# One stream of gate products laid between the products of three token mixers, and a merge that reads raw logits

## The chip, the cores and the metric

The kernel runs on one core of one Trainium2 chip. Its metric is the device time of one execution in microseconds (us). Five engines work side by side: PE (TensorE, matrix products), DVE (VectorE), ACT (ScalarE), POOL (GpSimd) and SP (SyncE, which here does nothing but issue transfers). They meet at semaphores only. SBUF is the on-chip memory and PSUM the accumulator memory that PE writes.

## The reference

One layer of a decoder trunk on 1024 tokens of width 1024, in f32. `h` is a normalised and modulated `x`; one projection `w_in` gives the inputs of four mixers and the logits of four gates; each mixer's output goes through its own branch weight, is gated and summed:

```python
h = rms_norm(x, g_mix[l]) * (1.0 + sc1) + sh1
(a_q, a_k, a_v, conv_in, c_q, c_k, c_v, c_r, c_low,
 d_q, d_k, d_v, gate_logits) = jnp.split(h @ w_in[l], split_points, axis=-1)
y_a = dilated_attention_mixer(a_q, a_k, a_v, q_gain[l], k_gain[l]) @ w_br_a[l]
y_b = conformer_conv_mixer(conv_in, ...) @ w_br_b[l]
y_c = gla_mixer(c_q, c_k, c_v, c_r, c_low, ...) @ w_br_c[l]
y_d = stick_breaking_mixer(d_q, d_k, d_v) @ w_br_d[l]
gates = jax.nn.sigmoid(gate_logits).reshape(bsz, seq, N_BRANCH, D_MODEL)
merged = (gates[:, :, 0] * y_a + gates[:, :, 1] * y_b
          + gates[:, :, 2] * y_c + gates[:, :, 3] * y_d)
x = x + gt1 * (merged @ w_out[l])
h = rms_norm(x, g_mlp[l]) * (1.0 + sc2) + sh2
x = x + gt2 * (jnp.square(jax.nn.relu(h @ w_up[l])) @ w_down[l])
```

The gate logits are 4 x 1024 columns, that is 32 tiles of 128 columns by 1024 tokens. The conv mixer has 256 channels, GLA 4 heads of 128 values with chunks of 64, stick-breaking 4 heads of 64, the dilated attention 3 groups of 4 heads of 64.

## The kernel before, in words

Every stage is one or more blocks. A block has one instruction list for each engine, written out by hand in the order in which it runs, and a barrier stands between two blocks: no engine begins the next block before all have left the last. So the order of the work is the order of the code, and a wait on a semaphore holds back all that stands behind it on its engine.

A product that has to be as exact as f32 is made of three f32r matmuls: both factors are split into a high and a low part, and `split_product` (L610) issues high x high, low x high and high x low. A dense tile is 128 columns of `w_in` (512 KB) times all of `h`. Its path is: SP loads it, ACT copies it to the high part (L132), POOL subtracts to get the low part (L136), PE makes two halves of 512 tokens with 8 x 3 = 24 matmuls of 128x512 each, ACT copies each half out of PSUM (L153), SP stores it. The class `Dense` does this for the 39 tiles of the projections during the front stage (0 to 506.5 us), with rings of two.

The stages then are, with their stretches in the profiled execution:

- window (dilated attention), block 1, 510.6 to 564.3 us: turns v by PE transposes, and for each of 12 tiles of q and k: squares on POOL, sums over the head on PE (into `ps_n`), ACT Ln (L1395) and Exp (L1398) into `wa_rinv`, DVE multiplies q or k by it (L1444). Ahead of the loop ACT is told which table of functions to load (L1389, `preload_act_table_set`).
- block 2, to 654 us: 24 units; 11 of them have two key tiles, 13 have one. PE: scores (L1493), transposes of the probabilities (L1504), values (L1514).
- block 3 (merging), 654.3 to 694.8 us: DVE merges the three groups, PE transposes, the result goes to `mix` in DRAM. Beside it two gate tiles (class `LastGates`).
- GLA: prepare to 738.8 us, with two more gate tiles; eight levels of masked products to 806.5 us (4 groups of 16 matmuls a level, L1889; two products and four masked copies a level on DVE, L1916, L1917, L1928); the state over 8 chunk pairs to 837.3 us; the norm to 873.0 us, for each head ACT L2023 (Square), L2024 to L2026 (Exp, Ln, Exp for the output gate), L2028 and L2029 (Ln, Exp of the mean square), and PE sums with `ones`.
- stick-breaking, 873.0 to 1036.1 us: a short block that turns v and scales q, then 24 steps, one for each half of the queries, key tile and head pair. A step has scores (L2136), sums with `ones` times an accumulated `later` (L2153) and with `reach` (L2156), values (L2170); DVE copies, adds to `later`, takes the argument; ACT makes Abs, Exp, Ln and a last Exp.
- merge, 1036.1 to 1467.0 us: for n = 0 to 7 and i = 0 to 3, PE makes the gate tile (48 matmuls, for the 28 tiles that no mixer has made) and then the branch product y (60 matmuls for one n over the four i); ACT takes the sigmoid from PSUM (L781), DVE multiplies and adds (L884, L889, L891), `merged` goes to DRAM. The branch weights of one n are loaded, split on ACT (L769) and POOL (L825).
- tail, from 1467 us: output product and MLP.

`recycle_semaphores` makes all semaphores free again and has barriers of its own.

Of the kernel before, what the change touches and what calls it, by code (L numbers as in the profile page):

```python
# [5 lines left out]
F32 = mybir.dt.float32  # L6
# [7 lines left out]
P = 128  # L14
# [60 lines left out]
class Dense:  # L75
# [3 lines left out]
    def __init__(self, nc, k, ctx, w_in):  # L79
# [16 lines left out]
        self.tiles = conv + stick + low + linear + window  # L96
        self.early = len(conv)

# [56 lines left out]
    def store(self, sp, j, h):  # L155
        column, width, row = self.tiles[j]
        sp.wait_ge(self.copied, NH * j + h + 1)
        sp.dma_start(self.k.proj[row * P:row * P + width, h * HALF:(h + 1) * HALF], self.out[0:width, h, :]).then_inc(self.stored[h], 16)
# [10 lines left out]
def stage_front(nc, k, dense, x, c, w_ada, b_ada, g_mix, g_mlp, conv_w, conv_b, ln_g, ln_b, b_gate, o_gain, q_gain, k_gain):  # L169
# [4 lines left out]
    N_TILES = len(dense.tiles)  # L174
# [13 lines left out]
    with ExitStack() as ctx:  # L188
# [78 lines left out]
        def _(sp):  # L267
# [33 lines left out]
            for j in range(dense.SLOTS, N_TILES):  # L301
# [9 lines left out]
            for j in range(N_TILES - 2, N_TILES):  # L311
                for h in range(NH):
                    dense.store(sp, j, h)
# [4 lines left out]
        def _(pool):  # L318
# [9 lines left out]
            for j in range(OPENING, N_TILES):  # L328
                dense.low(pool, j)

        @block.scalar
        def _(act):
# [56 lines left out]
            for j in range(2 * C, N_TILES):  # L389
                for h in range(NH):  # L390
                    dense.copy(act, j, h)
                if j + 2 < N_TILES:
                    dense.split(act, j + 2)
# [231 lines left out]
class LastGates:  # L625

    def __init__(self, nc, k, ctx, name, w_in, mixers):
        self.nc, self.k, self.mixers = nc, k, mixers  # L630
        self.w_view = w_in[0].rearrange("(t p) n -> p t n", p=P)
        self.raw = ctx.enter_context(nc.sbuf_tensor(f"{name}_raw", [P, 2, KT, P], F32))
        self.hi = ctx.enter_context(nc.sbuf_tensor(f"{name}_hi", [P, 2, KT, P], F32R))
        self.lo = ctx.enter_context(nc.sbuf_tensor(f"{name}_lo", [P, 2, KT, P], F32R))
        self.out = ctx.enter_context(nc.sbuf_tensor(f"{name}_out", [P, S], F32))
        self.loaded = sems(nc, ctx, f"{name}_in0", f"{name}_in1")
        self.hi_ready, self.lo_ready, self.done, self.copied, self.stored = sems(
            nc, ctx, *(f"{name}_{s}" for s in ("hi_ready", "lo_ready", "done", "copied", "stored")))

    def load(self, sp, j):  # L640
        if j >= 2:
            sp.wait_ge(self.lo_ready, j - 1)
        column = COL_GATES + (self.mixers[j] + 1) * D - P
        sp.dma_start(self.raw[:, j % 2], self.w_view[:, :, column:column + P]).then_inc(self.loaded[j % 2], 16)
# [1711 lines left out]
```

## Time and profile before

| | us |
|---|---|
| median of three runs | 2297.35 |
| the runs | 2296.37, 2302.18, 2297.35 |
| the profiled execution | 2296.16 |
| its span (first to last instruction) | 2294.4 |
| PE busy | 2105.6 (92%) |
| DVE, ACT, POOL busy | 957.6, 621.3, 562.1 |
| mean granted clock of PE | 0.958 of full |

1.8 us of the profiled execution lie outside its span. Busy time of PE is not its work: an f32r matmul of 128x512 is recorded with 0.39 us while the next one starts much earlier, so a stretch that is "busy" is one in which matmuls stand close together. The starts tell the pace. PEclk is the clock that was granted, as a share of 2.4 GHz; 0.5 is 1.2 GHz.

### The profile page before, as it was taken

The numbers are of one execution on the slowest core, as the hardware profiler recorded it, in microseconds if no ns is written. First come the engines' busy times: TensorE is split into PE (matmuls) and PEld (weight loads), VectorE is DVE, ScalarE is ACT, GpSimd is POOL, SyncE is SP. The second block draws the span as 40 slices with busy tenths as digits, with TensorE's granted clock in tenths as the row PEclk, the third lists the DMA queues.
The fourth block names the chain that finished last, engine by engine and source line by source line (L and its number), as shares of the span: only waits on it lengthen the run. The fifth ranks groups of instructions, "written<-read, shape, count | busy, mean of one in ns | idle before, by whom it ended". The sixth has DMA issues, their size and how long they took to land. (4 is left out here: it accounts for less than half of the span.)

```text
span 2294.4 us, 23961 instructions
## 1 busy us (share of the span) xinstructions
PE 2105.6 (92%) x9584; PEld 1666.5 (73%) x9584; DVE 957.6 (42%) x1146; ACT 621.3 (27%) x853; POOL 562.1 (24%) x258
## 2 busy tenths in 40 slices
PE   6999999986977676888999999689999999999999
PEld 5878888763865643326888888568888888888887
DVE  6365671018655924663111111345333333333334
ACT  5311111225732243553111111232222112122111
POOL 0212222216002400102222221120434334334332
PEclk9999999999988876998999999899999999999999
DMA  8345543233133011005222221340111111111112
GB/s 278 95 139 161 165 134 92 87 111 137 34 109 139 1 55 74 1 12 176 58 57 57 57 57 57 119 156 19 47 46 46 56 46 46 56 46 46 56 46 92
DMA packets 187865, 187.43 MB, mean 82 GB/s; under 512 B 7370, under 2 KB 154954, under 8 KB 187770
## 3 DMA queue, kind: packets, MB, share of 16 engines
q1 hardware_dynamic: 187600, 186.03, 25.7%
q8 instruction: 67, 1.10, 0.2%
q14 instruction: 28, 0.23, 0.0%
q10 hardware_dynamic: 170, 0.07, 0.0%
HBM read 148.17 MB, written 37.91 MB: 81 GB/s over the span
## 5 line engine op out<-in xcount | busy, mean ns | idle before, releaser
L617 PE MATMUL dn_ps<-h_hi,dn_hi 128*128 128x512 f32 (+1 forms) x608 | 240.5, 396 | 5.0 <-DVE h_lo L532 5.0
L619 PE MATMUL dn_ps<-h_hi,dn_lo 128*128 128x512 f32 (+1 forms) x608 | 237.3, 390 | 0.0
L618 PE MATMUL dn_ps<-h_lo,dn_hi 128*128 128x512 f32 (+1 forms) x608 | 237.1, 390 | 0.0
L1274 DVE TENSOR_TENSOR tl_x<-tl_x,tl_bank 128x512 f32<-128x512 f32 x256 | 173.3, 687 | 133.0 <-PE tl_bank L619 133.0
L1110 POOL TENSOR_TENSOR tl_w_lo<-tl_raw,tl_w_hi 128x1024 fp32r<-128x1024 f32 x64 | 153.5, 2399 | 228.4 <-ACT tl_w_hi L1031 228.4
L617 PE MATMUL tl_bank<-tl_h_hi,tl_w_hi 128*128 128x512 f32 x512 | 199.5, 390 | 0.0
L618 PE MATMUL tl_bank<-tl_h_lo,tl_w_hi 128*128 128x512 f32 x512 | 199.2, 389 | 0.0
L619 PE MATMUL tl_bank<-tl_h_hi,tl_w_lo 128*128 128x512 f32 x512 | 199.2, 389 | 0.0
L617 PE MATMUL tl_bank<-tl_w_hi,tl_u_hi 128*128 128x512 f32 x512 | 199.2, 389 | 0.0
L618 PE MATMUL tl_bank<-tl_w_lo,tl_u_hi 128*128 128x512 f32 x512 | 199.2, 389 | 0.0
L619 PE MATMUL tl_bank<-tl_w_hi,tl_u_lo 128*128 128x512 f32 x512 | 199.2, 389 | 0.0
L617 PE MATMUL mg_ps_g<-h_hi,mg_hi 128*128 128x512 f32 x448 | 175.4, 392 | 16.9 <-POOL mg_lo L822 16.9
L618 PE MATMUL mg_ps_g<-h_lo,mg_hi 128*128 128x512 f32 x448 | 175.2, 391 | 0.0
L619 PE MATMUL mg_ps_g<-h_hi,mg_lo 128*128 128x512 f32 x448 | 175.2, 391 | 0.0
L1116 POOL TENSOR_TENSOR tl_u_lo<-tl_square,tl_u_hi 128x1024 fp32r<-128x1024 f32 x32 | 104.5, 3266 | 277.2 <-DVE tl_square L1264 277.2
L136 POOL TENSOR_TENSOR dn_lo<-dn_raw,dn_hi 128x1024 fp32r<-128x1024 f32 (+1 forms) x37 | 87.4, 2365 | 327.7 <-ACT dn_hi L132 327.7
L1264 DVE TENSOR_TENSOR tl_square<-tl_relu 128x1024 f32<-128x1024 f32 x32 | 39.7, 1239 | 306.4 <-ACT tl_relu L1062 306.4
L822 POOL TENSOR_TENSOR mg_lo<-mg_raw,mg_hi 128x1024 fp32r<-128x1024 f32 x28 | 67.2, 2400 | 344.3 <-ACT mg_hi L763 344.3
L1031 ACT ACTIVATE tl_w_hi<-tl_raw 128x1024 fp32r<-128x1024 f32 x64 | 67.8, 1061 | 286.2 <-PE tl_bank L619 226.7
L617 PEld LDWEIGHTS dn_ps<-h_hi,dn_hi 128*128 128x128 f32 (+1 forms) x608 | 112.9, 186 | 31.0 <-DVE h_lo L532 6.2
L153 ACT ACTIVATE dn_out<-dn_ps 128x512 f32<-128x512 f32 (+1 forms) x74 | 44.3, 598 | 331.0 <-PE dn_ps L619 331.0
L889 DVE TENSOR_TENSOR mg_gate<-mg_ps_y,mg_gate 128x1024 f32<-128x1024 f32 x24 | 29.4, 1225 | 245.6 <-PE mg_ps_y L619 245.6
(313 smaller groups left out, 3900.0 us busy)
## 6 DMA issues: line engine op xcount, KB each, us to landing
ada<-w_ada_dram SPq DMA_DIRECT2D x24, 1024.0 KB, 7.5
dn_raw<-w_in_dram SPq DMA_DIRECT2D x38, 512.0 KB, 4.4
proj<-dn_out SPq DMA_DIRECT2D x72, 256.0 KB, 2.3
tl_raw<-w_up_dram SPq DMA_DIRECT2D x32, 512.0 KB, 3.8
tl_raw<-w_down_dram SPq DMA_DIRECT2D x32, 512.0 KB, 3.8
mg_raw<-w_in_dram SPq DMA_DIRECT2D x28, 512.0 KB, 4.6
wa_qk<-proj SPq DMA_DIRECT2D x6, 1024.0 KB, 17.4
mg_y_raw<-mix SPq DMA_DIRECT2D x10, 512.0 KB, 3.6
```

The source lines that it names most:

```text
L136: self.nc.gpsimd.tensor_tensor(self.lo_at(j), self.raw_at(j), self.hi_at(j).bitcast(F32), ALU.subtract).then_inc(self.lo_ready, 1)
L153: self.nc.scalar.activation(self.out[0:width, h, :], self.ps[0:width, h, :], ACT.Copy).then_inc(self.copied, 1)
L617: nc.tensor.matmul(out, w_hi[:, t, :], x_hi[:, t, :], start=begin, stop=False)
L618: nc.tensor.matmul(out, w_hi[:, t, :], x_lo[:, t, :], start=False, stop=False)
L619: mm = nc.tensor.matmul(out, w_lo[:, t, :], x_hi[:, t, :], start=False, stop=end)
L822: nc.gpsimd.tensor_tensor(g_lo[:, i % 2], g_raw[:, i % 2], g_hi[:, i % 2].bitcast(F32), ALU.subtract).then_inc(g_lo_ready, 1)
L889: nc.vector.tensor_tensor(gate[:, i % 2], y, gate[:, i % 2], ALU.mult).then_inc(gated, 1)
L1031: nc.scalar.activation(dst, raw[:, ring(j)], ACT.Copy).then_inc(hi_ready, 1)
L1110: nc.gpsimd.tensor_tensor(lo, raw[:, ring(j)], hi.bitcast(F32), ALU.subtract).then_inc(lo_ready, 1)
L1116: nc.gpsimd.tensor_tensor(u_lo[:, b % 2, f, :], square[:, n % 2], u_hi[:, b % 2, f, :].bitcast(F32), ALU.subtract).then_inc(u_lo_ready, 1)
L1264: nc.vector.tensor_tensor(square[:, n % 2], relu[:, n % 2], relu[:, n % 2], ALU.mult).then_inc(square_ready, 1)
L1274: nc.vector.tensor_tensor(x1[:, tt, cols], x1[:, tt, cols], bank[:, 4 + n % 4, :], ALU.add).then_inc(summed, 1)
```

## The change

All 32 gate tiles become tiles of `Dense`, behind the 39 of the projections, and are cut into pieces: a half is three pieces of 9, 9 and 6 matmuls (3, 3 and 2 of the 8 row tiles). `pieces(pe, n)` issues the next n of them, `serve` does ACT's part for a number of halves (the split of the next tile, the copy of this half), `lower` POOL's, `move` SP's (load the tile after the next, store the half). `LastGates` goes. 64 halves are dealt out so: window 6 (prepare), 8 (units), 4 (merging); GLA 8 (prepare), 8 (levels), 2 (state), 4 (norm); stick-breaking 20; merge 4. The mixers run in the order dilated attention, GLA, stick-breaking, as before. The logits go to DRAM raw, all 4 x 1024 rows.

```diff
-        self.tiles = conv + stick + low + linear + window
+        gates = [(COL_GATES + i * D + n * P, P, None) for n in range(D // P) for i in range(4)]
+        self.tiles = conv + stick + low + linear + window + gates
...
+    PARTS = (0, 3, 6, KT)
+    def pieces(self, pe, count):
+        for _ in range(count):
+            g, part = divmod(self.piece, 3)
+            j, h = self.first_gate + g // NH, g % NH
+            if part == 0:
+                pe.wait_ge(self.lo_ready, j + 1)
+                pe.wait_ge(self.copied, NH * (j - 1) + h + 1)
+            last = self.product(self.ps[:, h, :], j, h, self.PARTS[part], self.PARTS[part + 1])
+            if part == 2:
+                last.then_inc(self.done, 1)
+            self.piece += 1
+    def serve(self, act, halves):
+        while self.served < halves:
+            j, h = self.first_gate + self.served // NH, self.served % NH
+            if h == 0 and j + 1 < len(self.tiles):
+                self.split(act, j + 1)
+            self.copy(act, j, h)
+            self.served += 1
+    def move(self, sp, halves):
+        while self.moved < halves:
+            j, h = self.first_gate + self.moved // NH, self.moved % NH
+            if h == 0 and j + 2 < len(self.tiles):
+                self.load(sp, j + 2)
+            self.store(sp, j, h)
+            self.moved += 1
```

In the window's first block, the tables are no longer preloaded and Ln and Exp work in place in PSUM:

```diff
             def _(act):
-                nc.scalar.preload_act_table_set("natural_log_exp_and_others")
                 for t in range(2 * A_TILES):
+                    dense.serve(act, FROM + min(PREPARE, HEAD // 3 + t // 3))
                     act.wait_ge(summed, t + 1)
-                    nc.scalar.activation(rinv[:, t % 2], ps_n[:, t % 2, :, :].rearrange("p h c -> p (h c)"), ACT.Ln,
-                                         scale=1.0 / E, bias=k.eps[:, 0:1]).then_inc(logged, 1)
+                    nc.scalar.activation(sums, sums, ACT.Ln, scale=1.0 / E, bias=k.eps[:, 0:1]).then_inc(logged, 1)
                     act.wait_ge(logged, t + 1)
-                    nc.scalar.activation(rinv[:, t % 2], rinv[:, t % 2], ACT.Exp, scale=-0.5).then_inc(rooted, 1)
+                    nc.scalar.activation(sums, sums, ACT.Exp, scale=-0.5).then_inc(rooted, 1)
```

PE has 6 pieces ahead of the v transposes, then one behind each group of sums. In the units one piece stands between a unit's transposes and its values, and the scores have one PSUM buffer instead of two. In the merging block the mix store stands behind all of the block's `dense.move`. In GLA each of the first three of the four groups of a level is followed by a piece, the masked products have 3 PSUM buffers instead of 4, each head of the norm is preceded by two pieces. In stick-breaking the two blocks are one; the steps run head pair by head pair, the sums stay in one PSUM accumulator to which `pass_on` adds a product with `below`, so DVE's copies and adds to `later` go, and two pieces stand in each step:

```diff
+            dense.pieces(pe, HEAD)
...
+            for n in range(N + 3):
+                if n < N:
+                    scores(n)
+                if n < N + 2:
+                    dense.pieces(pe, 1)
+                if 2 <= n < N + 2:
+                    pass_on(n - 2)
+                if 1 <= n <= N:
+                    sums(n - 1)
+                if n < N + 2:
+                    dense.pieces(pe, 1)
+                if n >= 3:
+                    values(n - 3)
```

It also gets a `preload_act_table_set` of its own. In the merge, the gate products and their chain go; the logits are loaded into a ring of three, squashed in place, and the branch weights have two buffers:

```diff
+    GATE_RING = 3
+    Y_RING = 3
...
+            def load_branch(n):
+                if n == 1:
+                    sp.wait_ge(dense.done, NH * len(dense.tiles))
+                if n >= 2:
+                    sp.wait_ge(b_lo_ready, n - 1)
...
+            def load_logits(m):
+                if m < GATE_RING:
+                    sp.wait_ge(y_lo_ready, Y_TILES)
+                else:
+                    sp.wait_ge(used, m - GATE_RING + 1)
+                sp.dma_start(gate[:, m % GATE_RING], k.logits[m * P:(m + 1) * P, :]).then_inc(g_in[m % GATE_RING], 16)
...
+            for m in range(M):
+                load_logits(m)
+                if m % 4 == 2 and m >= 6:
+                    n = m // 4 - 1
+                    sp.wait_ge(used, 4 * n + 4)
+                    sp.dma_start(k.merged[n * P:(n + 1) * P, :], merged[:, n]).then_inc(stored, 16)
+                    if n + 2 < N_TILES:
+                        load_branch(n + 2)
...
+            for m in range(M):
+                squash(m)
+                if m == 0:
+                    split_branch(1)
+                if m % 4 == 3 and 1 <= m // 4 < N_TILES - 1:
+                    split_branch(m // 4 + 1)
...
+        def _(pe):
+            dense.pieces(pe, 3 * HALVES)
+            for m in range(M):
...
+                pe.wait_ge(b_lo_ready, n + 1)
```

Two more `recycle_semaphores` are in `build`, one behind the window stage and one behind the merge.

On ACT, in the window's first block, before (`wa_ps_n` holds the sums, `wa_rinv` the result):

```order
L1389 ACT_TABLE_LOAD
L1395 ACTIVATE wa_rinv<-wa_ps_n,eps 128x1024
L1398 ACTIVATE wa_rinv<-wa_rinv 128x1024
L1395 ACTIVATE wa_rinv<-wa_ps_n,eps 128x1024
L1398 ACTIVATE wa_rinv<-wa_rinv 128x1024
```

and now:

```order
L1328 ACT_TABLE_LOAD
L1328 ACTIVATE wa_ps_n<-wa_ps_n,eps 128x1024
L1330 ACT_TABLE_LOAD
L1330 ACTIVATE wa_ps_n<-wa_ps_n 128x1024
L135 ACTIVATE dn_hi<-dn_raw 128x1024
L156 ACTIVATE dn_out<-dn_ps 128x512
L1328 ACT_TABLE_LOAD
L1328 ACTIVATE wa_ps_n<-wa_ps_n,eps 128x1024
L1330 ACT_TABLE_LOAD
L1330 ACTIVATE wa_ps_n<-wa_ps_n 128x1024
```

One table load for the block has become one ahead of each Ln and one ahead of each Exp, 24 in the block; the gate stream's split and copy stand between.

On ACT, in the norm of GLA, one head, before:

```order
L2023 ACTIVATE gn_sq<-gl_oT 128x1024
L2024 ACTIVATE gn_sig<-gl_rT 128x1024
L2025 ACTIVATE gn_sig<-gn_sig 128x1024
L2026 ACTIVATE gn_sig<-gn_sig 128x1024
L2028 ACTIVATE gn_rinv<-gn_ps,eps 128x1024
L2029 ACTIVATE gn_rinv<-gn_rinv 128x1024
```

and now (`gl_att` and `gl_q` hold what `gn_sq`, `gn_rinv` and `gn_sig` held):

```order
L1972 ACTIVATE gl_att<-gl_oT 128x1024
L1973 ACTIVATE gl_q<-gl_rT 128x1024
L1974 ACT_TABLE_LOAD
L1974 ACTIVATE gl_q<-gl_q 128x1024
L1975 ACT_TABLE_LOAD
L1975 ACTIVATE gl_q<-gl_q 128x1024
L1977 ACT_TABLE_LOAD
L1977 ACTIVATE gl_att<-gn_ps,eps 128x1024
L1978 ACT_TABLE_LOAD
L1978 ACTIVATE gl_att<-gl_att 128x1024
```

Four loads have come in for each of the four heads; two more are in GLA's first block, and in the whole program there are 52 where there were 8.

On PE, in a step of stick-breaking, before (`sb_ps_z` scores, `sb_ps_c` sums, `sb_ps_o` values):

```order
L2136 MATMUL sb_ps_z<-sb_qk 128x384 x2
L2153 MATMUL sb_ps_c<-sb_later,ones 128x256
L2156 MATMUL sb_ps_c<-sb_softplus,reach 128x384
L2153 MATMUL sb_ps_c<-sb_later,ones 128x256
L2156 MATMUL sb_ps_c<-sb_softplus,reach 128x384
L2170 MATMUL sb_ps_o<-sb_weight,sb_v_tok 64x256 x2
```

and now, a sum, a piece of six matmuls of the gate stream (`dn_ps`) behind it, the values and the next scores:

```order
L2129 MATMUL sb_ps_c<-sb_softplus,sb_below 128x384 x2
L2119 MATMUL sb_ps_c<-sb_softplus,reach 128x512 x2
L663 MATMUL dn_ps<-h_hi,dn_hi 128x512
L664 MATMUL dn_ps<-h_lo,dn_hi 128x512
L665 MATMUL dn_ps<-h_hi,dn_lo 128x512
...
L2141 MATMUL sb_ps_o<-sb_weight,sb_v_tok 64x256 x2
L2105 MATMUL sb_ps_z<-sb_qk 128x256 x2
L663 MATMUL dn_ps<-h_hi,dn_hi 128x512
```

The gate matmuls that stood in the merge stand between the products of a step; the number of the step's own products is the same.

## Rows read from the trace of the kernel before

**Rows 1.** The page's first line.

```profile
span 2294.4 us, 23961 instructions
```

**Rows 2.** Stages: length; busy of PE, PEld, DVE, ACT, POOL; PEclk, DMA share, GB/s.

```profile
510.60:564.30 53.70, 32.91 (x96) 15.40 (x97) 46.02 (x38) 27.22 (x25) 37.85 (x16) 0.88 0.45 176
564.30:651.60 87.30, 83.50 (x612) 72.11 (x612) 57.60 (x95) 61.64 (x216) 0.00 (x0) 0.96 0.10 35
654.30:694.80 40.50, 26.00 (x112) 21.37 (x112) 18.13 (x23) 4.34 (x5) 4.73 (x2) 0.79 0.47 158
694.80:738.80 44.00, 38.85 (x152) 27.60 (x152) 24.93 (x19) 15.99 (x12) 8.22 (x3) 0.82 0.40 145
738.80:806.50 67.70, 45.12 (x512) 43.98 (x512) 66.04 (x59) 13.38 (x7) 29.75 (x17) 0.87 0.00 1
806.50:837.30 30.80, 30.13 (x176) 21.74 (x176) 4.12 (x14) 4.77 (x8) 0.00 (x0) 0.94 0.19 69
837.30:873.00 35.70, 15.12 (x16) 4.69 (x16) 14.58 (x12) 25.15 (x25) 0.00 (x0) 0.55 0.15 59
873.00:1036.10 163.10, 129.46 (x384) 59.36 (x384) 91.92 (x117) 78.54 (x96) 16.09 (x32) 0.87 0.08 26
1036.10:1467.00 430.90, 417.98 (x1824) 345.31 (x1824) 87.15 (x64) 81.10 (x79) 98.29 (x36) 0.98 0.26 72
```

**Rows 3.** PE in order of time in the merge: start, us, instruction, idle before.

```profile
1043.63 0.80 PE L617 MATMUL mg_ps_g<-h_hi,mg_hi 128*128 128x512 f32 x1 [16.86 <-POOL mg_lo L822]
...
1044.65 0.63 PE L619 MATMUL mg_ps_g<-h_hi,mg_lo 128*128 128x512 f32 x1
1045.08 0.63 PE L617 MATMUL mg_ps_g<-h_hi,mg_hi 128*128 128x512 f32 x1
...
1055.06 0.39 PE L617 MATMUL mg_ps_g<-h_hi,mg_hi 128*128 128x512 f32 x1
...
1056.88 0.39 PE L619 MATMUL mg_ps_g<-h_hi,mg_lo 128*128 128x512 f32 x1
```

**Rows 4.** ACT in order of time, late in the front stage.

```profile
453.90 1.28 ACT L399 ACT_TABLE_LOAD   x1
455.19 1.12 ACT L399 ACTIVATE cv_rinv<-fr_open_ps,eps 128x1024 f32<-128x1024 f32 x1
456.33 1.28 ACT L402 ACT_TABLE_LOAD   x1
457.62 1.06 ACT L402 ACTIVATE cv_rinv<-cv_rinv 128x1024 f32<-128x1024 f32 x1
```

**Rows 5.** PE in order of time, the window's first block.

```profile
515.99 9.93 PE L1410 MATMUL wa_ps_v<-ident,wa_vT 128*128 128x128 f32 x48 [9.29 <-DMA wa_vT<-proj]
```

**Rows 6.** GLA's levels in order of time: DVE, then PE.

```profile
761.04 5.02 DVE L1928 COPY_PREDICATED gl_att<-gl_mask,gl_ps_att 128x1024 f32<-128x1024 int32 x4
...
768.17 5.02 DVE L1928 COPY_PREDICATED gl_att<-gl_mask,gl_ps_att 128x1024 f32<-128x1024 int32 x4
...
769.67 5.29 PE L1889 MATMUL gl_ps_att<-gl_parts 64*128 64x128 f32 x64 [1.72 <-DVE gl_att L1928]
```

**Rows 7.** ACT in order of time in GLA's norm, one head.

```profile
851.91 1.06 ACT L2023 ACTIVATE gn_sq<-gl_oT 128x1024 f32<-128x1024 f32 x1
...
859.07 1.06 ACT L2023 ACTIVATE gn_sq<-gl_oT 128x1024 f32<-128x1024 f32 x1
```

**Rows 8.** PE in order of time in stick-breaking, one full step.

```profile
979.84 1.12 PE L2153 MATMUL sb_ps_c<-sb_later,ones 128*128 128x512 f32 x2
...
986.39 1.12 PE L2153 MATMUL sb_ps_c<-sb_later,ones 128*128 128x512 f32 x2
```

**Rows 9.** The low part of a branch weight on POOL: ns min/median/max.

```profile
L825 POOL TENSOR_TENSOR mg_br_lo<-mg_br_raw,mg_br_hi x8: 3893/3930/3945, 1047.6 to 1447.7; 128x1280 fp32r<-128x1280 f32 x8
```

**Rows 10.** Transfers by issue, with size and us to landing.

```profile
wa_qk<-proj SPq DMA_DIRECT2D x6, 1024.0 KB, 17.4
...
mg_raw<-logits SPq DMA_DIRECT2D x4, 512.0 KB, 4.2
```

More of the change, by code:

```diff
@@ L740, in store @@
-            def store(n):
-                sp.wait_ge(added, n * 3 + 3)
-                sp.dma_start(k.merged[bass.ds(n * P, P), :], merged[:, :]).then_inc(stored, 16)
-            def load_y(t0, t1):
-                for t in range(t0, t1):
-                    if t >= 2:
-                        sp.wait_ge(y_lo_ready, t - 1)
-                    sp.dma_start(y_raw[:, t % 2], k.mix[t * P:(t + 1) * P, :]).then_inc(y_in[t % 2], 16)
-            loads(0, first=True)
-            with sp.Fori(1, N_TILES - 1) as n:
-                loads(n)
@@ L753, in _, with load_y @@
-            loads(N_TILES - 1, last=True)
-            store(N_TILES - 1)
+            def load_y(t):
+                if t >= GATE_RING:
+                    sp.wait_ge(y_lo_ready, t - GATE_RING + 1)
+                sp.dma_start(gate[:, t % GATE_RING], k.mix[t * P:(t + 1) * P, :]).then_inc(y_in[t], 16)
+            def load_branch(n):
[3 more added lines that the diff above has]
+                    sp.wait_ge(b_lo_ready, n - 1)
+                for j in range(4):
+                    sp.dma_start(b_raw[n % 2][:, Y_FIRST[j]:Y_FIRST[j + 1], :],
+                                 w_br[j][0].rearrange("(t p) n -> p t n", p=P)[:, :, n * P:(n + 1) * P]).then_inc(b_in[n % 2], 16)
@@ L896, in _ @@
-            low_y(0, Y_EARLY)
-            body(0, first=True)
-            with dve.Fori(1, N_TILES) as n:
-                body(n)
+            for t in range(Y_TILES):
+                dve.wait_ge(y_hi_ready, t + 1)
+                nc.vector.tensor_tensor(k.y_lo[:, t, :], gate[:, t % GATE_RING], k.y_hi[:, t, :].bitcast(F32), ALU.subtract).then_inc(y_lo_ready, 1)
+            for m in range(M):
+                n, i = m // 4, m % 4
+                dve.wait_ge(gate_ready, m + 1)
+                dve.wait_ge(y_done, m + 1)
+                y = ps_y[:, m % Y_RING, :, :].rearrange("p h c -> p (h c)")
+                g = gate[:, m % GATE_RING]
+                if i == 0:
+                    nc.vector.tensor_tensor(merged[:, n], y, g, ALU.mult).then_inc(used, 1)
+                else:
+                    nc.vector.tensor_tensor(g, y, g, ALU.mult).then_inc(gated, 1)
+                    dve.wait_ge(gated, m - n)
+                    dve.wait_ge(used, m)
+                    nc.vector.tensor_tensor(merged[:, n], merged[:, n], g, ALU.add).then_inc(used, 1)
@@ L1675, in _ @@
                 last.then_inc(turned, 1)
-            for j in range(2, len(GATES_IN_WINDOW)):
-                pe.wait_ge(gates.copied, j - 1)
-                gates.product(pe, j, ps_g[:, j % 2])
+            dense.pieces(pe, 3)
 GLA_HEADS = 4
@@ L1754, in _ @@
                     last.then_inc(turned, 1)
[L1755 to L1758 removed]
+                dense.pieces(pe, 3 * (PREPARE - 1) - HEAD)
                 pe.wait_ge(dve_step, 7)
```

890 lines of the change are left out of this document (396 added, 494 removed).

## The prediction

> **What bounds the kernel now.** I read the stages first. The span is 2294.4 us [rows 1], and the changed stages fill 510.6 to 1467.0 of it [rows 2]; front and tail keep their instructions. In the merge PE is busy for 417.98 of 430.90 us at a clock of 0.98, so the merge is PE's work and nothing else. In the other rows of that group PE leaves room: prepare of the window 32.91 of 53.70, levels 45.12 of 67.70, norm 15.12 of 35.70, stick-breaking 129.46 of 163.10. Then I read who fills those: DVE has 46.02 in the window's prepare and 66.04 of 67.70 in the levels, ACT 25.15 of 35.70 in the norm. The units (83.50 of 87.30) and the state (30.13 of 30.80) have no room.
>
> Next the pace of PE, from starts and not from busy time [rows 3]. At full clock (2.4 GHz) eight starts lie between 1055.06 and 1056.88, 0.2275 us for one f32r matmul of 128x512. At half clock (1.2 GHz), after 16.86 us in which PE was idle, it is 0.43 (1044.65 to 1045.08). So a half of a gate tile, 24 matmuls, is 5.46 us, a piece 1.82 on average, and a cold start costs some 2 us more, for about eleven matmuls.
>
> **What goes.** The merge loses 28 tiles x 48 = 1344 matmuls, 305.8 us. What it keeps is 480 matmuls of y, 109.2 us, and it gets 4 halves, 21.8 us, plus 2 for a cold start. At its old pace it had 415.0 us of matmuls in 430.9.
>
> New waits in the merge: body n+2 needs its branch weight, whose chain hangs on the last logits of body n+1. In body n+1 the first gated product is done 12 matmuls (2.7) and one DVE operation (1.2, estimated from the 1.25 of a masked copy of the same size, 5.02 for four [rows 6]) after its start; then the load of logits, 4.2 [rows 10] with a store and a branch weight ahead of it in the queue, so 5 to 6; a sigmoid and the split, 1.1 and 1.3 (estimates from ACT's 1.06 for 1024 elements [rows 4]); POOL 3.93 [rows 9]. Together about 15.5 after the start of the body, which is only 13.7 of matmuls long. I take 2 us for each of seven bodies, 14, and 3 for the first logits, which can be fetched only when all of y is split. The merge: 21.8 + 2 + 109.2 + 14 + 3 = 150, a change of **-281**. Below, if the chain hides, -295; above, see the rivals.
>
> **What the mixers get.** 56 more halves less what was there: they had 8 (the four early tiles) and get 60, so 52 x 5.46 = 284 us go in. What each stage can hide:
>
> - Window prepare: 6 halves, and 24 table loads on ACT. Where Ln and Exp alternate with a load before each, the trace has load 1.28, Ln 1.12, load 1.28, Exp 1.06, end to start [rows 4]: from 453.90 to 458.68, 4.8 us. Twelve tiles make 57.6, more than PE's sums (32.91 less 9.93 over twelve, 1.9 a tile [rows 2, 5]) and a piece (1.82), so ACT is the bound. It begins late: six pieces first, 10.9 plus 2 cold from 511, which hides the 9.29 wait for v; then a third of the v transposes, 3.3 [rows 5], and a tile's sums, to 529. Add 57.6 and some 4 for splits and copies of the stream: 591 in place of 564.3, **+27**. With the loads at nothing the block would be bound by PE at +17.
> - Units: 24 pieces, 43.7 us. PE is idle for 3.8 of the stretch and its clock 0.96 may rise to 1.0, worth 3.3 of 83.50 [rows 2]. 43.7 - 3.8 - 3.3 = **+37**. The single score buffer costs nothing if a piece stands in the wait for DVE; if not, it takes from the hidden part only.
> - Window merging: four halves as before. The last pieces and their store stand ahead of the mix store, 3.5, and there is one more recycling, 2 (an estimate: the gap between the blocks of the units and of the merging is 2.7 [rows 2]). **+5.5**.
> - GLA prepare: 8 halves for 4, +21.8; idle there 5.2. One or two table loads. **+18**.
> - Levels: now DVE's 7.13 (761.04 to 768.17) for a level; PE needs 5.3 of its own and 3 pieces, 5.46, and becomes the bound at 10.7 [rows 6]. The masks on DVE still hold the first copies back (761.04 less one level is 753.9, 15.1 after the start), then comes what is left of the first level, 5, and seven more: 15.1 + 5 + 7 x 10.7 = 95 for 67.7, **+27**.
> - State: six pieces between saturated products, **+11**.
> - Norm: a head takes 7.16 on ACT [rows 7]; four loads add 4 x 1.28 = 5.12, less 0.7 in which ACT now waits for the sums (7.16 less six activations of near 1.07), plus the stream's copies: 11.7 a head. Four heads, **+20**. PE's 21.8 of pieces go beside that; without the loads this stage would gain or lose about 1.
> - Stick-breaking: 20 halves, 109.2 us. A full step is 6.55 on PE [rows 8] with scores, four sums and values back to back, and the 24 steps hold 18 full steps' worth of columns, 118. Then v's transposes 3.3, about 6 for some 54 switches between the two kinds of product (0.1 each, my guess, bounds 0 and 16), 9.4 from the last product to the merge as now: 109.2 + 118 + 3.3 + 6 + 9.4 = 246, against 163.1 **+84**. From a step's scores to its sum there are two DVE operations (1.25 each) and three of ACT (1.06 each), 6 us with waking; PE has three pieces, the sums before, the values and the next scores to do in that time, 11.
> - Tail: one more recycling, **+2**.
>
> Sum: 27 + 37 + 5.5 + 18 + 27 + 11 + 20 + 84 + 2 - 281 = -49.5. Against the profiled execution, 2296.16, that is 2246.7. The median of the runs is 1.2 us above that execution, so **2248**.
>
> **A rule against it.** The rows show a load of 1.28 us and the next ACT instruction at its end, with nothing between [rows 4]. The Trainium skill, ScalarE: Activation LUTs, section What ACT_TABLE_LOAD costs, adds about 1.38 us of draining to each switch, 2.66 in all; in this trace that does not show. By it, 40 loads on the path would cost 55 us more.
> The same page, section Table sets: the hidden batching unit, says that Ln and Exp share one set, so that a pair should need one load; the program's order shows one for each all the same.
>
> **The rivals.**
>
> 1. The loads or the pieces hide better than I think. For it: ACT in the levels and in stick-breaking has room, and a load can run before its wait ends. Against it: in Ln-Exp chains there is no wait to hide in. Without the loads' cost on the path, -10 in the prepare and -18 in the norm, 2220; with two of the merge's stalls gone too, 2213. Chance 0.17.
> 2. A rival on the slow side: the ring of three logits bounds the merge. For one m, the time is (L + 4.5)/3, where L is a load's landing and 4.5 the sigmoid, two DVE operations and waking. PE needs 109.2/32 = 3.4 for one m, so it decides from L = 5.8 on, and eats the whole gain of 49.5 from L = 12: 32 x (12 + 4.5)/3 = 176, where my sum has 126. For it: 1 MB loads took 17.4 when the queue was full [rows 10]; the merge reads 0.5 MB for logits each 3.4 us plus weights and stores, near 250 GB/s. Against it: the same load took 4.2. At L = 14, 32 x 18.5/3 = 197, +71, so 2319. Chance 0.05.
> 3. Each switch costs 2.66 on the path, by the sum above: 24 and 16 loads more by 1.38, +55, so 2303: no gain. Only a stall behind each load, which the rows don't have, would do that. Chance 0.04.
> 4. The pieces break the mixers' chains: a piece is issued whole, and PE waits in it for `lo_ready` or `copied`, with the mixer's products queued behind. If ACT serves a half late by 1 us in each of the 60, +50 to +60 and the gain is gone: 2300. For it: ACT's list puts a copy behind a mixer's waits in each stage. Against: a half has three pieces of slack and two PSUM banks. Chance 0.08.
>
> **How the numbers follow.** My own case has 0.66, with 2215 to 2285. A measurement of this kernel can tell about 0.3%, 7 us, from no change. Faster by more than that: 0.17 and 0.64 of my 0.66, 0.81. Within: its last 0.02 and 0.05 of rivals 3 and 4, which end close to no change, 0.07. Slower: the other 0.07 of these and rival 2, 0.12. The range reaches past rival 1, by the bounds of the guessed terms (16 for the switches, 14 for the stalls), and up to 2290: 2205 to 2290.
>
> **What would show it.** The merge near 150 us with PE waiting for the branch weight's low part at each body; 24 loads of 1.28 between Ln and Exp and PE idle there; the levels at 10.7 a level with DVE waiting for PE; a step of stick-breaking of 10.2. I am wrong if PE stands idle within the stick steps, if a load is followed by a gap, if the logits land later than 6 us, or if the clock of the mixers stays below 0.9.

## The result: slower by 1.9%, and where the time went

The changed kernel takes 2344.79 us (median; 2342.97 to 2348.71) against 2296.86 of the kernel before beside it: the ratio is 1.0193, 95% interval 1.016 to 1.0227. It is 48 us slower where 49 us faster was forecast. The profiled execution has a span of 2346.9 us, 52.5 more than before [rows 1]; it is the slowest of the four executions, 3.9 above their median.

The page's PE line has 2139.7 us busy where it had 2105.6, and 9584 matmuls as before. The same number of products is made, so the question is where PE stood idle or ran at half clock. The view by stage says it; its columns are those of [rows 2], kernel after:

```profile
514.50:598.80 84.30, 65.93 (x240) 42.91 (x240) 26.52 (x38) 62.12 (x57) 35.87 (x19) 0.96 0.40 147
598.80:729.80 131.00, 126.64 (x804) 106.55 (x804) 62.05 (x97) 70.21 (x228) 9.57 (x4) 0.99 0.20 60
729.80:775.20 45.40, 27.42 (x112) 22.54 (x112) 18.57 (x23) 4.56 (x7) 4.79 (x3) 0.80 0.44 141
775.20:836.30 61.10, 58.88 (x248) 45.18 (x248) 22.54 (x19) 23.06 (x22) 12.61 (x5) 0.93 0.41 135
836.30:947.40 111.10, 102.55 (x704) 83.77 (x705) 72.30 (x59) 21.84 (x19) 37.90 (x21) 0.94 0.14 41
947.40:989.50 42.10, 41.21 (x224) 30.63 (x224) 4.13 (x14) 6.70 (x11) 2.36 (x1) 0.95 0.22 76
989.50:1047.70 58.20, 36.72 (x112) 24.59 (x112) 18.88 (x12) 49.64 (x46) 4.71 (x2) 0.79 0.22 72
1047.70:1346.20 298.50, 244.31 (x864) 152.59 (x864) 75.69 (x80) 99.46 (x127) 38.34 (x44) 0.89 0.16 50
1346.20:1522.30 176.10, 146.70 (x576) 117.25 (x576) 93.49 (x66) 57.20 (x56) 25.80 (x9) 0.90 0.57 185
```

Taking each stage from its first instruction to the first of the next, before and after:

| stage | before | after | change | forecast |
|---|---|---|---|---|
| front | 510.6 | 514.5 | +3.9 | 0 |
| window prepare | 53.7 | 84.7 | +31.0 | +27 |
| units | 90.4 | 130.6 | +40.2 | +37 |
| window merging | 40.1 | 45.4 | +5.3 | +5.5 |
| GLA prepare | 44.1 | 61.7 | +17.6 | +18 |
| levels | 67.6 | 110.5 | +42.9 | +27 |
| state and norm | 66.5 | 100.3 | +33.8 | +31 |
| stick-breaking | 163.6 | 298.5 | +134.9 | +84 |
| merge | 436.4 | 176.1 | -260.3 | -281 |
| tail | 821.4 | 824.6 | +3.2 | +2 |

Three stages hold 87.5 of the 102 us between forecast and result: stick-breaking (51), the merge (21) and the levels (16).

**Stick-breaking.** The view of waits of that stage names one wait of PE above all (us in total, times, longest), kernel after:

```profile
PE dn_ps L663 <- POOL dn_lo L139: 45.1, 7, 8.3
```

PE stands before a piece because the tile's low part is not there. In order of time around one of the seven (start, us, engine, instruction), kernel after:

```profile
1079.20 1.05 ACT L135 ACTIVATE dn_hi<-dn_raw 128x1024 fp32r<-128x1024 f32 x1
1079.36 0.41 POOL L2245 TENSOR_SCALAR_AFFINE_SELECT sb_weight<-sb_weight 128x256 f32<-128x256 f32 x1 [5.65 <-ACT sb_weight L2228]
...
1080.25 1.98 PE L2105 MATMUL sb_ps_z<-sb_qk 64*128 64x512 f32 x4
1080.64 0.41 POOL L2245 TENSOR_SCALAR_AFFINE_SELECT sb_softplus<-sb_softplus 128x256 f32<-128x256 f32 x1 [0.88 <-DVE sb_softplus L2182]
...
1086.67 0.61 ACT L2228 ACTIVATE sb_weight<-sb_weight 128x512 f32<-128x512 f32 x1
...
1087.35 0.41 POOL L2245 TENSOR_SCALAR_AFFINE_SELECT sb_weight<-sb_weight 128x256 f32<-128x256 f32 x1 [6.30 <-ACT sb_weight L2228]
1087.72 2.34 POOL L139 TENSOR_TENSOR dn_lo<-dn_raw,dn_hi 128x1024 fp32r<-128x1024 f32 x1
...
1090.11 0.79 PE L663 MATMUL dn_ps<-h_hi,dn_hi 128*128 128x512 f32 x1 [7.88 <-POOL dn_lo L139]
1090.70 0.63 PE L664 MATMUL dn_ps<-h_lo,dn_hi 128*128 128x512 f32 x1
```

ACT has the high part ready at 1080.25, and POOL needs 2.34 us for the low part. But POOL's list has a mask of the weights first, and that waits for ACT's Exp of a later turn of the loop, which ends at 1087.28. The low part comes 7.5 us after it could, POOL is idle for 6.30 of them, and when PE goes on its first matmuls are 0.43 to 0.59 apart where full clock has 0.2275: half clock. Six of the seven waits last 6.5 to 8.3 us; the seventh lasts 0.8, and behind it PE goes on at full clock.

**Merge.** The same pattern at a body's start, PE, then ACT, then POOL, kernel after:

```profile
1446.40 0.39 PE L665 MATMUL mg_ps_y<-y_hi,mg_br_lo 128*128 128x512 f32 x1
1451.58 0.79 PE L663 MATMUL mg_ps_y<-y_hi,mg_br_hi 128*128 128x512 f32 x1 [4.79 <-POOL mg_br_lo L775]
```

```profile
1446.34 1.06 ACT L756 ACTIVATE mg_gate<-mg_gate 128x1024 f32<-128x1024 f32 x1 [4.38 <-DMA mg_gate<-logits]
1447.31 1.25 ACT L748 ACTIVATE mg_br_hi<-mg_br_raw 128x1280 fp32r<-128x1280 f32 x1
```

```profile
1448.63 2.89 POOL L775 TENSOR_TENSOR mg_br_lo<-mg_br_raw,mg_br_hi 128x1280 fp32r<-128x1280 f32 x1 [15.90 <-ACT mg_br_hi L748]
```

The split of the branch weight stands behind the sigmoid of the last logits, and those land late: the body has ended (1446.40) before its successor's weight is split. It happens at three bodies, every second one, 4.2 to 4.8 us each with half clock behind it, and POOL's part is 2.9, where [rows 9] had 3.93. Two more waits of that size stand at the merge's start, one for the low part of y and one for DVE's first gated product (L815), which hangs on the first logits. PE's waits of the stage, kernel after:

```profile
PE mg_ps_y L663 <- POOL mg_br_lo L775: 13.7, 3, 4.8
PE dn_ps L663 <- PEq L60: 8.9, 1, 8.9
PE mg_ps_y L663 <- DVE y_lo L807: 4.8, 1, 4.8
PE mg_ps_y L663 <- DVE mg_merged L815: 4.1, 1, 4.1
```

The 8.9 is the time between PE's last piece in stick-breaking and its first in the merge, and lies in the stage before. Ahead of the wait for the low part of y, ACT stands before a copy of the gate stream, whose buffer is still being stored, with y's split behind it, kernel after:

```profile
1378.31 0.60 ACT L156 ACTIVATE dn_out<-dn_ps 128x512 f32<-128x512 f32 x1 [7.88 <-DMA logits<-dn_out]
1378.81 2.94 ACT L752 ACTIVATE y_hi<-mg_gate 128x1024 fp32r<-128x1024 f32 x3
```

**Table loads.** ACT in the window's first block, kernel after:

```profile
562.54 1.28 ACT L1328 ACT_TABLE_LOAD   x1
563.83 1.09 ACT L1328 ACTIVATE wa_ps_n<-wa_ps_n,eps 128x1024 f32<-128x1024 f32 x1
564.94 1.28 ACT L1330 ACT_TABLE_LOAD   x1
566.23 1.01 ACT L1330 ACTIVATE wa_ps_n<-wa_ps_n 128x1024 f32<-128x1024 f32 x1
567.15 0.59 ACT L156 ACTIVATE dn_out<-dn_ps 128x512 f32<-128x512 f32 x1
567.77 1.28 ACT L1328 ACT_TABLE_LOAD   x1
```

Everything is end to start as in [rows 4]; a tile takes 4.7 us, or 5.2 with a copy of the stream. There is no gap beside a load. The trace has 50 loads in the whole program, not the 52 named ahead of the prediction; 24 and 16 of them are those of this block and of the norm.

### The profile page after: what moved, and what is told of

Read it like the earlier page. It is cut to its first block and busy times, and to the rows that moved or that the text cites. A ratio compares the mean times of both kernels' runs of the same rounds, so it can differ in the third digit from the quotient of the medians.

```text
span 2346.9 us, 23858 instructions
## 1 busy us (share of the span) xinstructions
PE 2139.7 (91%) x9584; PEld 1683.4 (72%) x9584; DVE 940.5 (40%) x1109; ACT 704.8 (30%) x955; POOL 541.3 (23%) x260
## 5 line engine op out<-in xcount | busy, mean ns | idle before, releaser
L663 PE MATMUL dn_ps<-h_hi,dn_hi 128*128 128x512 f32 (+1 forms) x1120 | 479.3, 428 | 86.0 <-POOL dn_lo L139 45.1
L664 PE MATMUL dn_ps<-h_lo,dn_hi 128*128 128x512 f32 (+1 forms) x1120 | 449.5, 401 | 0.0
L665 PE MATMUL dn_ps<-h_hi,dn_lo 128*128 128x512 f32 (+1 forms) x1120 | 449.2, 401 | 0.0
L663 PEld LDWEIGHTS dn_ps<-h_hi,dn_hi 128*128 128x128 f32 (+1 forms) x1120 | 217.4, 194 | 162.4 <-issue 59.7
L139 POOL TENSOR_TENSOR dn_lo<-dn_raw,dn_hi 128x1024 fp32r<-128x1024 f32 (+1 forms) x69 | 165.2, 2395 | 721.2 <-ACT dn_hi L135 721.2
L664 PEld LDWEIGHTS dn_ps<-h_lo,dn_hi 128*128 128x128 f32 (+1 forms) x1120 | 217.7, 194 | 51.2 <-issue 7.8
L665 PEld LDWEIGHTS dn_ps<-h_hi,dn_lo 128*128 128x128 f32 (+1 forms) x1120 | 216.5, 193 | 50.7
L663 PEld LDWEIGHTS tl_bank<-tl_h_hi,tl_w_hi 128*128 128x128 f32 x512 | 96.1, 188 | 20.0
L665 PEld LDWEIGHTS tl_bank<-tl_h_hi,tl_w_lo 128*128 128x128 f32 x512 | 96.1, 188 | 20.0
L664 PEld LDWEIGHTS tl_bank<-tl_w_lo,tl_u_hi 128*128 128x128 f32 x512 | 96.1, 188 | 20.0
```

The costliest lines, as they stand in the source:

```text
L139: self.nc.gpsimd.tensor_tensor(self.lo_at(j), self.raw_at(j), self.hi_at(j).bitcast(F32), ALU.subtract).then_inc(self.lo_ready, 1)
L663: nc.tensor.matmul(out, w_hi[:, t, :], x_hi[:, t, :], start=begin, stop=False)
L664: nc.tensor.matmul(out, w_hi[:, t, :], x_lo[:, t, :], start=False, stop=False)
L665: mm = nc.tensor.matmul(out, w_lo[:, t, :], x_hi[:, t, :], start=False, stop=end)
```

## The experiments

The first four are repairs of the changed kernel, one cause each and then all three. A ratio is always to the kernel before as timed beside the run. That kernel's medians there were 2302.94 (first four), 2303.43 (next four), 2297.83 (the next two) and 2313.16 (the last two), with single executions from 2292.61 to 2322.65, and its 2296.86 above is the lowest. So gains are read from one changed kernel to the next. The changed kernel itself, timed again, came within 2.7 us, and of a difference smaller than that nothing is concluded.

**POOL's list in stick-breaking.**

```diff
             for n in range(N + 1):
-                dense.lower(pool, FROM + halves_before(n - 1) if n else FROM + 1)
+                dense.lower(pool, FROM + halves_before(n))
```

> The changed kernel (2344.8 us) with POOL's list in stick-breaking shifted by one step: the low part of the next gate tile stands ahead of the step's two masks instead of behind them. Theory A (POOL's list holds the low part back: seven waits of PE for dn_lo, 45.1 us in sum, and about 2 us of half clock behind each): the waits go and stick-breaking falls from 298.5 to about 240 us, the whole to about 2288. Theory B (the excess in stick-breaking comes from the switches between f32 and f32r products and from PE's own work, the low part is only the last of several late things): stick-breaking stays within 10 us of 298.5, the whole near 2340.

Measured: 2290.38 us (2286.69 to 2294.83), 54 less than the changed kernel; ratio to the kernel before 0.9938 (0.9913 to 0.9962). The same wait and the stage:

```profile
PE dn_ps L663 <- POOL dn_lo L139: 3.4, 5, 0.8
```

```profile
1046.40:1289.40 243.00, 230.59 (x864) 142.91 (x864) 77.66 (x80) 99.48 (x127) 38.84 (x44) 0.98 0.20 61
```

The stage falls from 298.5 to 243.0 and PE's clock in it rises from 0.89 to 0.98. The waits give 41.7 of the 55.5; the rest, 13.8, is 2.3 for each of the six long ones, if all of it is the half clock behind them. The five waits that are left last 0.5 to 0.8 us. Theory A holds in its number too. This one line turns a loss of 1.9% into about level: 0.6% faster than the kernel before as timed beside it, 0.3% against its 2296.86.

**The table preload of the window's first block.**

```diff
             def _(act):
+                nc.scalar.preload_act_table_set("natural_log_exp_and_others")
                 for t in range(2 * A_TILES):
```

> The changed kernel with the table preload of the window's first block put back, which takes the program's table loads from 52 to 10. Theory A (each of the 24 and 16 loads costs its 1.28 us on the path): the window's first block falls from 84.3 to about 68 us (then bound by PE), the norm of GLA from 58.2 to about 40, the whole by 30 to 40 us, to about 2310. Theory B (a switch also drains for 1.38 us): twice that, about 2270. Theory C (the loads run in ACT's idle time): within 7 us of 2344.8.

Measured: 2309.90 us (2308.39 to 2312.37), 35 less. The window's prepare falls from 84.7 to 71.3, state and norm together from 100.3 to 82.4. The trace has 9 loads where the changed kernel's has 50: of 43 in the mixers two are left, the one asked for here and the one that stick-breaking asks for, since no function between them needs another table. The 40 loads of the two stages are 51 us of ACT, and the two stages give 31.3: not each load was on the path in full. In the prepare stage PE becomes the bound, and the stage stays 17.6 over the kernel before, where the forecast had +17 without the loads. The whole fits theory A's number (2310); B, twice that, and C, nothing, fall.

**The branch weights of the merge.** Loaded as soon as their buffer is free, split two tiles earlier:

```diff
+                if m % 4 == 0 and m >= 4 and m // 4 + 1 < N_TILES:
+                    load_branch(m // 4 + 1)
                 if m % 4 == 2 and m >= 6:
...
-                    if n + 2 < N_TILES:
-                        load_branch(n + 2)
...
-                if m % 4 == 3 and 1 <= m // 4 < N_TILES - 1:
+                if m % 4 == 1 and 1 <= m // 4 < N_TILES - 1:
```

> The changed kernel with the branch weights of the merge fetched four tiles earlier and split two tiles earlier. Theory A (a body waits for the low part of its branch weight, which hangs on the last logits of the body before: four or five waits of 4.5 to 5.2 us, each followed by half clock): the merge falls from 176.1 to about 150 us, the whole to about 2319. Theory B (the ring of three logits is what is short, the branch weight only happens to come last): the waits move to the logits and the merge stays above 168 us.

Measured: 2325.37 us (2320.99 to 2326.58), 19 less, 6 above theory A's number; the merge falls from 176.1 to 153.9. No wait for the branch weight is left in the view, and two waits of 4.8 us at the merge's start stay (for the low part of y, and for the first gated product). The ring of three logits is not what bounds it, so theory B falls. The stage gives 22.2 us for three waits of 13.7 in sum, so 8.5 beyond the waits themselves, 2.8 for each.

**All three.**

> All three of the edits before together. If the three causes are separate the gains add up: 57 + 35 + 26 us off 2344.8, about 2227, which is under the kernel before (2296.9). If they share one cause or give each other room (a faster norm makes the stream late elsewhere), it stays above 2250.

Measured: 2232.53 us (2231.37 to 2233.97), ratio 0.9693 (0.9644 to 0.9742). That is 112 less than the changed kernel, where 54 + 35 + 19 = 108 was the sum of the single ones: the gains add up, so the causes are separate as far as 4 us can tell. The three stages, in the order units, stick-breaking, merge:

```profile
583.30:713.90 130.60, 126.59 (x804) 106.23 (x804) 62.01 (x96) 70.22 (x228) 9.57 (x4) 0.99 0.19 59
1012.60:1255.30 242.70, 230.31 (x864) 142.65 (x864) 77.65 (x80) 99.48 (x127) 38.86 (x44) 0.98 0.20 61
1255.30:1406.30 151.00, 137.12 (x576) 111.73 (x576) 98.26 (x66) 57.34 (x56) 25.99 (x9) 0.95 0.65 216
```

Stick-breaking is 3 us under the forecast's 246. That the merge has 151 where the forecast had 150 is luck: that sum held 14 us of waits for the branch weight, and this kernel has none.

The next four start from this kernel.

**The levels' pieces in one place.**

```diff
-                        if m < 3:
-                            dense.pieces(pe, 1)
+                        if m == 0:
+                            dense.pieces(pe, 3)
```

> The kernel with all three repairs (2232.5 us), and in GLA's levels the three pieces of a level stand together behind the first group of products instead of one behind each of three groups. Theory A (going from f32 products to a piece and back costs PE some 0.7 us: a piece of nine lasts 2.26 where nine matmuls are 2.05, and a group of 16 products 1.64 where 16 more in a row add 1.11): 16 trips fewer, the levels fall by about 12 us from 109 and the whole to about 2221. Theory B (the levels are long because DVE's masked copies and the three score buffers wait in turns with PE): a lump leaves DVE idle longer, the levels stay or grow, 2232 or more.

Measured: 2218.72 us (2217.03 to 2221.95), 13.8 less; the levels fall from 109.2 (110.4 to 110.6 in the next three kernels) to 98.7. First PE in the levels of the changed kernel, then of this one (rows between are left out):

```profile
895.42 2.82 PE L1827 MATMUL gl_ps_att<-gl_parts 64*128 64x128 f32 x32
898.17 0.50 PE L663 MATMUL dn_ps<-h_hi,dn_hi 128*128 128x512 f32 x1
...
900.43 1.71 PE L1827 MATMUL gl_ps_att<-gl_parts 64*128 64x128 f32 x16
902.07 0.50 PE L663 MATMUL dn_ps<-h_hi,dn_hi 128*128 128x512 f32 x1
...
904.35 1.71 PE L1827 MATMUL gl_ps_att<-gl_parts 64*128 64x128 f32 x16
...
907.57 2.82 PE L1827 MATMUL gl_ps_att<-gl_parts 64*128 64x128 f32 x32
910.32 0.50 PE L663 MATMUL dn_ps<-h_hi,dn_hi 128*128 128x512 f32 x1
```

```profile
882.64 5.03 PE L1828 MATMUL gl_ps_att<-gl_parts 64*128 64x128 f32 x64
887.61 0.50 PE L663 MATMUL dn_ps<-h_hi,dn_hi 128*128 128x512 f32 x1
...
893.27 2.04 PE L1828 MATMUL gl_ps_att<-gl_parts 64*128 64x128 f32 x22
```

In the changed kernel the last group of a level and the first of the next stand together. A level lasts 12.15 us (895.42 to 907.57), and 10.63 with one lump (882.64 to 893.27): 1.52 for two trips fewer, 0.76 a trip. The rows say where it goes. A group of 16 products alone takes 1.64 us (900.43 to 902.07), while 16 more in a row add 1.11 (32 take 2.75, 907.57 to 910.32), so a group that stands alone costs 0.53 more. A piece of nine takes 2.28 (902.07 to 904.35), where nine matmuls at 0.2275 are 2.05, so 0.23 more. PE waits for nobody in these rows; its one wait for DVE is in the first level (6.3 us in the changed kernel, 8.8 here), which the lump does not shorten. Seven levels at 1.52 are 10.6, the 10.5 of the stage. So the trip costs 0.76, and not the 0.66 that a division by all 16 trips gives. Theory B falls. The other 3.3 of the 13.8 us lie outside the levels, 2.0 of them in state and norm (82.4 to 80.4), and are not explained.

**Stick-breaking's pieces in one place.**

```diff
                 if n < N + 2:
-                    dense.pieces(pe, 1)
+                    dense.pieces(pe, 2)
...
-                if n < N + 2:
-                    dense.pieces(pe, 1)
                 if n >= 3:
                     values(n - 3)
```

> The kernel with all three repairs, and in stick-breaking the two pieces of a step stand together behind the scores. Theory A (a trip between the kinds of product costs 0.7 us): 26 trips fewer, 12 to 18 us less in stick-breaking (242.7), the whole about 2217. Theory B (the second piece covers the time from the softplus to the sum, or from the argument to the values): PE gets waits on ACT and DVE, the same or slower, 2232 to 2245.

Measured: 2234.27 us (2232.37 to 2240.41), no change, and the stage has 242.6 against 242.7. Theory A fails here. Theory B's waits do not appear either: within the steps PE has only the five short waits for the low part, 3.6 us in all as before. A change between pieces and these products shows no cost. All the trips taken away here lie between a piece and products that take in 128 rows (the sums and the values), while the levels' products take in 64 (`64*128` in the rows), two halves of the rows in turn. Whether the rows, the size or the number of the small products makes the price was not tried.

**Stick-breaking without pieces.** `HEAD, EACH = 0, 0`, and the twenty halves are made in the merge.

> The kernel with all three repairs, with stick-breaking's 20 halves made in the merge instead (24 halves there, 109.2 us more). Says what stick-breaking hides. If its own work is bound by PE (118 us of columns), as the forecast took it, the stage falls by 100 to 110 us and the whole stays within 10 us of 2232. If its chain through ACT and DVE is what bounds it alone, as in the kernel before (163 us), it falls only to about 150 and the whole rises to about 2250.

Measured: 2252.72 us (2251.03 to 2257.60), 20.2 more. The stage, its steps alone, and PE's longest wait in it:

```profile
1014.00:1163.00 149.00, 124.79 (x384) 55.44 (x384) 72.68 (x80) 79.70 (x97) 17.88 (x34) 0.91 0.09 29
1031.00:1154.00 123.00, 115.69 (x353) 48.97 (x353) 67.23 (x71) 75.28 (x90) 16.98 (x31) 0.98 0.00 1
```

```profile
PE sb_ps_z L2095 <- DMA sb_vT<-proj: 11.1, 1, 11.1
```

The stage alone takes 149 us, and with 109.2 us of pieces 242.7: they cost 93.6 there, 15.6 are hidden. In the merge they cost 114.3. The number is that of the expectation's second theory, but its reason does not hold: the steps take 123 us with PE busy for 115.7 of them, and PE waits there for POOL's masks (6.2 us in eight waits) and hardly for ACT or DVE (1.3 us in three waits). What the pieces hide is above all the load that opens the stage, 11.1 us of waiting for v and 1.6 for q. Between the steps there is little to fill. The rewritten stage by itself is 14.5 shorter than the old one (163.6).

**The mix stores ahead of the last logits.**

```diff
-            dense.move(sp, FROM + PREPARE + DURING + MERGING)
+            dense.move(sp, FROM + PREPARE + DURING + MERGING - 1)
             sp.wait_ge(copied, 4)
             sp.dma_start(feature_tiles(k.mix[Y_A * P:Y_B * P, :]), yT[:, :, :]).then_inc(stored, 16)
+            dense.move(sp, FROM + PREPARE + DURING + MERGING)
```

and the same in stick-breaking.

> The kernel with all three repairs, and the mix store of the window's merging and of stick-breaking stands ahead of the last store of logits instead of behind it. Theory A (the mix store waits there for the last half and its landing ends the block): 2 to 4 us less in each of the two stages, about 2226. Theory B (the last store of logits, which follows PE's last piece, ends the block either way): within 2 us of 2232.5.

Measured: 2224.21 us (2222.05 to 2225.48), 8.3 less. Window merging falls from 45.5 to 40.7, more than theory A's 2 to 4, and stick-breaking from 242.7 to 239.7. The two are 7.8 of the 8.3. Theory A holds, B falls.

**Both.** 

> The kernel with all three repairs, the lump in the levels (13.8 us less by itself) and the earlier mix stores (8.3 less by itself) together. They are in different stages, so they should add: 2232.5 - 22 = 2210, under every kernel so far. If they share a wait: 2217 or more.

Measured: 2211.84 us (2207.38 to 2217.58), ratio 0.9609 (0.9563 to 0.9656): 20.7 less, near the sum of the two (22.1).

**Two pieces after every other unit.** 

```diff
-                    if n < UNIT_PIECES:
-                        dense.pieces(pe, 1)
+                    if n < UNIT_PIECES and n % 2 == 0:
+                        dense.pieces(pe, 2)
```

> The one before, and in the window's units two pieces after every other unit's transposes instead of one after each. Theory A (a trip from small f32 products to a piece and back costs 0.66 us, as in the levels): 12 trips fewer, the units fall from 130 to about 122 us, the whole to 2202. Theory B (the unit's values wait for the copy of the transposed probabilities, which the piece covers, so the units without a piece get a wait): no gain, 2210 or up to 10 more.

Measured: 2213.02 us (2210.83 to 2214.44); units 131.8 against 132.0 (129.1 to 132.0 in all profiles without this edit, so 8 us would show). No gain: that is theory B's number, but not its reason, since PE waits for no copy here (1.3 us in all, for DVE). Again the products on both sides of a piece, transposes and values, take in 128 rows. So the trip's cost is not general, and small products alone do not bring it: these are 128x128 and 128x64.

**The front's store.** In the changed kernel SP issues the store of the conv mixer's output behind the last dense store, at 508.58; here at 487.27:

```diff
+                if j == N_TILES - 1:
+                    sp.wait_ge(cv_out, C)
+                    sp.dma_start(feature_tiles(k.mix[Y_B * P:Y_C * P, :]), acc[:, :, :]).then_inc(cv_stored, 16)
```

```profile
508.58 0.44 SPq L359 DMA_DIRECT2D mix<-cv_acc  x1
```

```profile
487.27 0.43 SPq L360 DMA_DIRECT2D mix<-cv_acc  x1
```

> The best kernel so far (repairs, lump in the levels, earlier mix stores: 2211.8 us) with the front stage's store of the conv mixer's output put back to where the kernel before has it, two tiles of stores earlier. Theory A (that store, issued at 508.58 behind the last dense store where the kernel before issued it at 486.0, lands last and holds the block open): the front stage is 3 to 4 us shorter, the whole about 2208. Theory B (the front's 3.9 us more come from the longer half clock at its start): no change beyond 2 us.

Measured: 2210.66 us (2204.78 to 2213.36), ratio 0.9575 (0.9532 to 0.9618). The front is 512.7 against 515.4. In the twelve profiles with the store in its late place the front is 513.7 to 515.4, so the edit takes off 1 us or more, and less than the 3 to 4 of theory A. The whole differs by 1.2 us, less than the spread, and does not decide it. It is the lowest median here, level with the one before it.

**The changed kernel again.** 

> The changed kernel unaltered, on the same chip and in the same call as the best one, for a direct comparison: 2345 us within 4, that is about 134 us over the best kernel.

Measured: 2347.48 us (2342.48 to 2349.58), ratio 1.0167 (1.0121 to 1.0213): 137 us over the kernel above, and 2.7 from its own first median, as expected.

## Why the prediction was wrong

The steps that held: what the merge loses (305.8 us of matmuls) and what it keeps; the units, the window's merging block, GLA's prepare, the state; the table loads. The load pairs were put at 4.8 us a tile and take 4.7; the window's prepare, and state and norm together, came within 4 us of the forecast. The experiment that takes the loads out gives 35 us, where the two terms held 28. Three sums are off by a little: stick-breaking's 246 is 83 over 163.1, not 84; four heads at 11.7 for 7.16 are 18, not 20; and rival 1's 2213 takes off 7 us for two stalls of 2.

**The step that failed** is the overlap in stick-breaking. It is the sentence that from a step's scores to its sum there are 6 us of DVE and ACT while PE has 11 of work, which left no wait of PE in a step. For DVE and ACT it holds: with POOL's list in order PE has no wait for them in the steps. But it looked at two of the three engines that serve a step. POOL has the masks of the diagonal steps and, in the new order, the low parts behind them. A mask that waits for ACT held back the low part, and the low part held back PE. The term was put at nothing; it is 41.7 us of waits and 13.8 more behind them. The stage's sum of 246 us was right to 3 us once POOL's list was put in order (243.0). It held 6 for the switches between the two kinds of product, which show no cost there, so part of that nearness is luck. Rival 4 had the form of it (a piece waits for `lo_ready` with the mixer's products behind) and a size of 50 to 60; it blamed ACT's list, and its case against, two PSUM banks and three pieces of slack, says nothing about a low part. It should have had POOL's list written beside PE's, and a far higher chance.

**The merge**: the step that named the branch weight's chain was right in place and wrong in size. It had 2 us for each of seven bodies, 14; the three waits and what follows them are 22.2 by the experiment, so 8 more. The larger part is at the merge's start. There the forecast had 2 for a cold start and 3 for the first logits. With the weights early, PE's last matmul of the merge ends 147.4 us after the first begins, for 131.0 of matmuls: 16.4, so 11 more. Two waits of 4.8 are in it (for the low part of y, and for the first gated product); the rest, some 6, goes with the half clock of the start. The trace puts the first wait down to ACT's list, where a copy of the gate stream stands ahead of y's split. No experiment took either wait away, so this is read from the trace and not shown. Rival 2 (the ring of logits) is out: with the weights early the merge is 153.9.

**The levels**: 10.7 us a level were forecast from 5.3 of own work and 5.46 of pieces; the changed kernel takes 12.15, and 10.63 with one trip a level. So the two further trips of each level, 1.52, are what the sum lacked: over seven levels 10.6 of the 16 us. The term for a trip, guessed at 0.1 in stick-breaking with bounds 0 and 16 in sum, was not carried into the levels at all. The rest is in the first level, where the first masked copy stands 17.6 us after the stage's start (854.48) and the forecast had 15.1, and in some 3 us that no run divides.

**The small ones**: 3.9 in the front was not looked at, since its instructions were taken to be the same; one of its stores was moved behind another, which is worth 1 us or more of it. At 500 us PE is four matmuls, 0.9 us, behind the kernel before; why is open. Rival 3, a load that costs more than its 1.28 us on the path, does not hold here: the rows have 1.28 and the next instruction at its end, and 41 loads fewer give 35 us. A drain of 1.38 us behind each, the figure of The Trainium skill, ScalarE: Activation LUTs, section What ACT_TABLE_LOAD costs, would by estimate have made the block's tile 7.5 us, where the trace has 4.7. That Ln and Exp share one set (The Trainium skill, ScalarE: Activation LUTs, section Table sets: the hidden batching unit) is borne out here when the set is asked for by name: with it the block has one load, without it 24.

The sum of what was missed is +51 +21 +16 +14 (the rest of the table) = 102, which is the distance between 2246.7 and 2348.7 in the profiled executions.

## What to carry to other kernels

When work is laid into another stage's gaps, write down the list of every engine that touches it, the small helper engines too: a queue runs in order, and a wait in it that has nothing to do with your work delays it. A wait of PE can cost more than itself: here six of 6.5 to 8.3 us cost about 2.3 each in half clock behind them, and three of 4.2 to 4.8 about 2.8. And ask what a stage can hide before filling it, and where: stick-breaking had room for 16 us of the 109 given to it, most of it at its opening load and not between its steps. Look for lines that go with a rewrite, too: one lost line of table preload cost 35 us.

## What the runs showed of the hardware

In the levels a change between small f32 products (64x128, on 64 rows) and f32r products of 128x512 costs PE 0.76 us there and back. Beside products on 128 rows, in stick-breaking and in the window's units, no cost shows (26 and 12 trips fewer gave nothing that the spread lets show). A table set with both Ln and Exp, asked for once, served every stage from the window's first block to the end of GLA: no load in between, where there were 42. POOL's subtraction of a branch weight took 2.9 us in the new merge, where it was 3.93 in the old one [rows 9]; what made it faster was not tried.
